# The second layer norm of a mixture-of-experts block, taken one token tile at a time

## What is computed

```python
def layer_norm(x, g, b):
    mu = jnp.mean(xf, -1, keepdims=True)
    var = jnp.mean(jnp.square(xf - mu), -1, keepdims=True)
    return (xf - mu) * lax.rsqrt(var + LN_EPS) * g + b

for l in range(DEPTH):                       # DEPTH = 2
    mix = hybrid_mixer(x, ...)
    x = layer_norm(DEEPNORM_ALPHA * x + mix, ln1_g[l], ln1_b[l])
    moe = hier_moe(x, ...)
    x = layer_norm(DEEPNORM_ALPHA * x + moe, ln2_g[l], ln2_b[l])
return x
```

## Time and profile before

| | |
|---|---|
| median of 3 runs | 1804.32 us (1799.9 to 1805.04) |
| the profiled execution, its own time | 1798.07 us |
| its span | 1795.9 us |
| mean granted TensorE clock | 0.991 |
| TensorE matmul busy | 1741.9 us, 97% |
| VectorE busy | 853.6 us, 48% |
| ScalarE busy | 639.0 us, 36% |
| GpSimd busy | 143.4 us, 8% |

### The profile page before, as it was taken

How to read it: one execution, slowest core, us unless ns; L and a number is a source line. 1 busy time by engine, 2 the same in 40 slices (tenths; PEclk the granted TensorE clock), 3 DMA queues, 4 the chain that set the end, 5 groups by cost and what they waited for, 6 DMA issues and landing times. The chain is left out here.

```text
span 1795.9 us, 24264 instructions
## 1 busy us (share of the span) xinstructions
PE 1741.9 (97%) x9930; PEld 1317.1 (73%) x9930; DVE 853.6 (48%) x1332; ACT 639.0 (36%) x859; POOL 143.4 (8%) x190
## 2 busy tenths in 40 slices
PE   9999999999999999999999999999989999999996
PEld 6888789998988879999888854444458986544442
DVE  6575654445556565444576461122147854312223
ACT  4456443334363544333445221111124541211110
POOL 1020001111111001111110010000002001000000
PEclk9999999999999999999999999999999999999998
DMA  8544545554544454553753169999964506799992
GB/s 302 183 141 148 180 142 188 186 188 168 184 163 141 164 172 158 187 187 117 245 168 117 49 236 399 402 401 396 358 191 148 176 1 245 298 401 399 395 402 110
DMA packets 150941, 396.63 MB, mean 221 GB/s; under 512 B 19376, under 2 KB 83888, under 8 KB 126256
## 3 DMA queue, kind: packets, MB, share of 16 engines
q1 hardware_dynamic: 150832, 395.16, 59.9%
HBM read 394.08 MB, written 1.05 MB: 220 GB/s over the span
## 5 line engine op out<-in xcount | busy, mean ns | idle before, releaser
L803 PE MATMUL ps<-split,split 128*128 128x256 f32 (+3 forms) x1872 | 631.5, 337 | 15.4 <-DVE split L796 4.7
L807 PE MATMUL ps<-split,split 128*128 128x256 f32 (+3 forms) x1872 | 627.9, 335 | 0.6 <-DVE split L2035 0.6
L804 PE MATMUL ps<-split,split 128*128 128x256 f32 (+3 forms) x1872 | 625.0, 334 | 0.0
L781 DVE TENSOR_TENSOR split<-ring,split 128x2048 fp32r<-128x2048 f32 x137 | 314.6, 2304 | 261.7 <-ACT split L774 261.7
L803 PEld LDWEIGHTS ps<-split,split 128*128 128x128 f32 x1872 | 352.4, 188 | 51.2 <-issue 12.0
L807 PEld LDWEIGHTS ps<-split,split 128*128 128x128 f32 x1872 | 352.8, 188 | 34.9 <-DVE split L2035 1.5
L804 PEld LDWEIGHTS ps<-split,split 128*128 128x128 f32 x1872 | 353.9, 189 | 33.1 <-issue 0.5
L774 ACT ACTIVATE split<-ring 128x2048 fp32r<-128x2048 f32 x137 | 262.0, 1916 | 284.6 <-PE ps L807 277.2
L2620 DVE SCALAR_TENSOR_TENSOR arena<-arena,ps 128x256 f32<-128x256 f32 x32 | 15.4, 480 | 226.2 <-ACT arena L1968 226.2
L796 DVE TENSOR_TENSOR split<-ring,split 128x1536 fp32r<-128x1536 f32 (+3 forms) x44 | 80.9, 1852 | 32.1 <-ACT split L790 31.9
L790 ACT ACTIVATE split<-ring 128x1536 fp32r<-128x1536 f32 (+3 forms) x44 | 67.8, 1548 | 76.7 <-PE ps L807 73.2
(11 more groups left out here) (245 smaller groups left out, 2018.2 us busy)
## 6 DMA issues: line engine op xcount, KB each, us to landing
ring<-in_w_in SPq DMA_DIRECT2D x52, 1024.0 KB, 4.9
ring<-in_w_gate_up SPq DMA_DIRECT2D x44, 1024.0 KB, 5.3
ring<-in_expert_w_gate SPq DMA_DIRECT2D x32, 1024.0 KB, 7.7
ring<-in_expert_w_up SPq DMA_DIRECT2D x32, 1024.0 KB, 9.9
ring<-in_expert_w_down SPq DMA_DIRECT2D x32, 1024.0 KB, 10.9
ring<-in_w_down SPq DMA_DIRECT2D x22, 1024.0 KB, 4.9
ring<-in_w_in SPq DMA_DIRECT2D x28, 768.0 KB, 4.7
high<-in_expert_w_gate SPq DMA_DIRECT2D x16, 1024.0 KB, 7.3
```

Source lines behind the costliest of these rows:

```text
L781: nc.vector.tensor_tensor(split(slot), slot, split(high[:, n % HIGH, :]), ALU.subtract).then_inc(low_done.sem, 1)
L803: nc.tensor.matmul(acc, sh, mh, start=start, stop=False)
L804: nc.tensor.matmul(acc, *second, start=False, stop=False)
L807: return nc.tensor.matmul(acc, *third, start=False, stop=stop)
```

## The change

It touches only the second norm. `add_scattered` now holds the four additions, and is called behind the branch: with `last` true in the `If` body. An addition is a `tensor_tensor_reduce`, which also leaves the row's sum; the second half row of a tile starts from the sum of the first. A `tensor_scalar` makes minus the mean of it. ScalarE squares `H - mean` over the whole row, with the sum of squares as by-product. GpSimd makes variance plus epsilon and the power -1/2 for each tile by itself. `second_norm` does both `scalar_tensor_tensor` steps of tile 0 and then both of tile 1, through a buffer `centred` of its own. The idle matmuls at the seam go from 20 to 14. At the tail SP issues `H` in two transfers, one for each tile. Four small buffers are added, and the semaphores change to suit. The first norm keeps its form.

```diff
@@ -482,6 +482,10 @@
         hT = carve(2, 2 * P)
+        centred = carve(TT, D)
+        row_sum = carve(TT, 2)
+        less_mean = carve(TT)
+        square_sum = carve(TT)
 
@@ -554,7 +558,8 @@
         passed = sem("passed")
-        mean_done = signal("mean_done", 2)
+        mean_done = signal("mean_done", 1)
+        mean_in = signal("mean_in", TT)
         table_done = sem("table_done")
@@ -591,9 +596,9 @@
         mix_done = signal("mix_done", 4)
-        stat_done = signal("stat_done", 2)
-        rstd_done = signal("rstd_done", 2)
-        gained = signal("gained", 4)
+        stat_done = signal("stat_done", 1 + TT)
+        rstd_done = signal("rstd_done", 1 + TT)
+        gained = signal("gained", TT)
         wo_in = signal("wo_in", 4)
@@ -619,7 +624,8 @@
         sc_added = signal("sc_added", 4)
-        moe_moments = signal("moe_moments", 4)
+        centred_in = signal("centred_in", TT)
+        squares_in = signal("squares_in", TT)
 
@@ -1006,9 +1012,10 @@
 
-            sp_.wait_ge(x_ready.sem, x_ready.at(LAYERS, 0))
-            sp_.dma_start(out.rearrange("b (t p) d -> (b p) t d", p=P), H[:]).then_inc(out_done, 16)
-            sp_.wait_ge(out_done, 16)
+            for t in range(TT):
+                sp_.wait_ge(x_ready.sem, x_ready.at(LAYERS, t + 1 - TT))
+                sp_.dma_start(out.rearrange("b (t p) d -> (b p) t d", p=P)[:, t, :], H[:, t, :]).then_inc(out_done, 16)
+            sp_.wait_ge(out_done, 16 * TT)
 
@@ -1684,7 +1691,7 @@
                         if l < LAYERS - 1:
-                            keep_running(bank2(("yg", 0, 0, 0)), 20)
+                            keep_running(bank2(("yg", 0, 0, 0)), 14)
                     with pe.Else():
@@ -1991,6 +1998,11 @@
                 more_passes(1)
+                for t in range(TT):
+                    act.wait_ge(mean_in.sem, mean_in.at(l, t + 1))
+                    nc.scalar.activation(flat(XG[1][:, 4 * t:4 * t + 4, :]), H[:, t, :], ACT.Square,
+                                         bias=less_mean[:, t:t + 1],
+                                         accum_out=square_sum[:, t:t + 1]).then_inc(squares_in.sem, 1)
 
@@ -2477,20 +2489,20 @@
 
-                def layer_norm(buf, n):
+                def layer_norm(buf):
 
                     for t in range(TT):
                         last = nc.vector.bn_aggr(mv2[:, t, :], moments2[:, t, :, :])
                     last.then_inc(mean_done.sem, 1)
-                    dve.wait_ge(mean_done.sem, mean_done.at(l, n + 1))
+                    dve.wait_ge(mean_done.sem, mean_done.at(l, 1))
                     nc.vector.tensor_scalar(rstd2, mv2[:, :, 1], LN_EPS, None, ALU.add).then_inc(stat_done.sem, 1)
                     for t in range(TT):
                         nc.vector.scalar_tensor_tensor(out=H[:, t, :], in0=buf[:, t, :], scalar=mv2[:, t, 0:1],
                                                        in1=lng[:, 0, :], op0=ALU.subtract,
                                                        op1=ALU.mult).then_inc(gained.sem, 1)
-                    dve.wait_ge(rstd_done.sem, rstd_done.at(l, n + 1))
+                    dve.wait_ge(rstd_done.sem, rstd_done.at(l, 1))
                     for t in range(TT):
-                        dve.wait_ge(gained.sem, gained.at(l, 2 * n + t + 1))
+                        dve.wait_ge(gained.sem, gained.at(l, t + 1))
                         nc.vector.scalar_tensor_tensor(out=H[:, t, :], in0=H[:, t, :], scalar=rstd2[:, t:t + 1],
@@ -2499,7 +2511,7 @@
                 step(last)
-                layer_norm(H, 0)
+                layer_norm(H)
                 for kp in (1, 3):
@@ -2630,27 +2642,50 @@
                             turned_picks(d + 1)
+                    return passes
+
+                def add_scattered(pass_, last):
+
+                    lp = l * PASSES + pass_
                     dve.wait_ge(resid_in.sem, resid_in.at(l, TT))
+                    if last:
+                        dve.wait_ge(ln2_in.sem, ln2_in.at(l, 32))
+                        dve.sem_inc(passed, 1)
                     for i in range(4):
-                        t, cols = i // 2, slice(i % 2 * 512, (i % 2 + 1) * 512)
-                        nc.vector.tensor_tensor(H[:, t, cols], content_p("sc", i), H[:, t, cols],
-                                                ALU.add).then_inc(sc_added.sem, 1)
-                        dve.wait_ge(sc_added.sem, sc_added.at(lp, i + 1))
-                        moments_of(H, i).then_inc(moe_moments.sem, 1)
-                    return passes
-
-                def second_norm(done):
-
-                    dve.wait_ge(moe_moments.sem, moe_moments.at(PASSES * l + done - 1, 4))
-                    wait_apart(dve, ln2_in.sem, ln2_in.at(l, 32))
-                    layer_norm(H, 1)
+                        t, a = divmod(i, 2)
+                        cols = slice(a * 512, (a + 1) * 512)
+                        key = ("sc", 0, i)
+                        dve.wait_ge(filled[banks2[key]], in_pass(key, l, pass_) + 1)
+                        if a == 1:
+                            dve.wait_ge(sc_added.sem, sc_added.at(lp, i))
+                            dve.sem_inc(passed, 1)
+                        nc.vector.tensor_tensor_reduce(H[:, t, cols], bank2(key), H[:, t, cols], 1.0,
+                                                       0.0 if a == 0 else row_sum[:, t, 0:1], ALU.add, ALU.add,
+                                                       row_sum[:, t, a:a + 1]).then_inc(sc_added.sem, 1)
+                        if last and a == 1:
+                            dve.wait_ge(sc_added.sem, sc_added.at(lp, i + 1))
+                            nc.vector.tensor_scalar(less_mean[:, t:t + 1], row_sum[:, t, 1:2], -1.0 / D, None,
+                                                    ALU.mult).then_inc(mean_in.sem, 1)
+
+                def second_norm():
+
+                    for t in range(TT):
+                        dve.wait_ge(mean_in.sem, mean_in.at(l, t + 1))
+                        nc.vector.scalar_tensor_tensor(out=centred[:, t, :], in0=H[:, t, :], scalar=less_mean[:, t:t + 1],
+                                                       in1=lng[:, 0, :], op0=ALU.add,
+                                                       op1=ALU.mult).then_inc(centred_in.sem, 1)
+                        dve.wait_ge(centred_in.sem, centred_in.at(l, t + 1))
+                        wait_apart(dve, rstd_done.sem, rstd_done.at(l, 1 + t + 1))
+                        nc.vector.scalar_tensor_tensor(out=H[:, t, :], in0=centred[:, t, :], scalar=rstd2[:, t:t + 1],
+                                                       in1=lng[:, 1, :], op0=ALU.mult,
+                                                       op1=ALU.add).then_inc(x_ready.sem, 1)
                     if l < LAYERS - 1:
                         head_low(l + 1)
 
                 def skip_pass(n):
 
                     dve.drain()
-                    for signal_ in (xg_dve, pT_in, h2_done, y_low, sc_added, moe_moments):
+                    for signal_ in (xg_dve, pT_in, h2_done, y_low, sc_added):
                         dve.sem_inc(signal_.sem, n * signal_.per)
@@ -2660,14 +2695,17 @@
                     with dve.If(passes <= done):
-                        second_norm(done)
+                        add_scattered(done - 1, True)
+                        second_norm()
                         skip_pass(PASSES - done)
                     with dve.Else():
+                        add_scattered(done - 1, False)
                         moe_pass(done)
                         if done + 1 < PASSES:
                             more_passes(done + 1)
                         else:
-                            second_norm(PASSES)
+                            add_scattered(done, True)
+                            second_norm()
 
@@ -2770,16 +2808,21 @@
                 diagonal(nm, nm_masked)
-                for n in range(2):
-                    wait_apart(pool, stat_done.sem, stat_done.at(l, n + 1))
-                    nc.gpsimd.tensor_tensor(rstd2, rstd2, minus_half[:, 0:2], ALU.pow).then_inc(rstd_done.sem, 1)
-                    if n == 0:
-                        for t in range(TT):
-                            wait_apart(pool, split_high.sem, split_high.at(l, t + 1))
-                            nc.gpsimd.tensor_tensor(in_blocks(moe_split(H_low[:, t, :])),
-                                                    H[:, t, :].rearrange("p (n k) -> p k n", k=KT),
-                                                    in_blocks(moe_split(H_high[:, t, :])),
-                                                    ALU.subtract).then_inc(split_low.sem, 1)
+                wait_apart(pool, stat_done.sem, stat_done.at(l, 1))
+                nc.gpsimd.tensor_tensor(rstd2, rstd2, minus_half[:, 0:2], ALU.pow).then_inc(rstd_done.sem, 1)
+                for t in range(TT):
+                    wait_apart(pool, split_high.sem, split_high.at(l, t + 1))
```

(11 more changed lines are left out.)

## The result

| | before | after |
|---|---|---|
| median | 1804.43 us (5 runs, 1799.9 to 1805.04) | 1790.67 us (5 runs, 1788.54 to 1791.97) |
| ratio | | 0.9925, 95% interval 0.9911 to 0.9940 |
| profiled execution | 1798.07 us, span 1795.9 | 1789.22 us, span 1787.5 |

The change is faster by 13.8 us, 0.75%. One execution among all that follow, of f3, took 7542.34 us and is left out of its median.

What follows compares the result with a forecast made beforehand. TensorE, busy for 97% of the span, was taken as the bound, leaving two norm stretches of 10.8 us. Tail 2.7 plus seam 1.6 gave 4.3 us; from the median 1804.32, 1800.0 us, range 1794.5 to 1804.5.

Steps and rivals of the forecast that it cites:

- The norm: Second norm at seam and tail: both tiles ready 1.5 us earlier (0.9 to 2.1), tile 0 about 3 us earlier.
- The tail: End of the kernel: 1.5 us from the norm plus 1.2 from the halved output transfer, together 2.7 us (0.9 to 3.4).
- The seam's start: Start of products at the seam: 2.1 us earlier, 1.5 from the norm and 0.6 beyond, worth 1.3 to 2.1.
- The sum behind it: Seam, norm to first product: VectorE's low part of 1.39 us, then a low half of 0.62 twice, about 2.2 us.
- The clock: TensorE at the seam: if its clock falls as before, first products run at 1.2 GHz longer, losing 0.5 to 0.8 us.
- So the whole picture shifts: Behind the seam: VectorE's jump and SP's transfers all come earlier, so 1.6 us arrives further on (-1 to +4).
- the two pauses: VectorE behind the seam's jump: 6.37 us ahead of L2294, 4.69 ahead of L2296, taken as code fetches and expected as before.
- the 4.3 us forecast: Whole kernel: tail's 2.7 us plus seam's 1.6 us, making 1798.07 us 1793.8 for an execution like the profiled one.
- B: Rival at the seam: earlier start lets a fetch precede weight loads, a 4.69 us pause goes; 9.0 us gained, 1795.3; chance 0.17.
- E: Rival, VectorE behind the seam's jump: longer code falls differently into fetches, two more pauses add 11.1 us, 1811.1; chance 0.07.
- The rule on the shared ports: VectorE and GpSimd in the norm: their shared port pair is an exclusive lock, so VectorE would be held up as well.
- Rival D: Both norms: short steps slower than priced, GpSimd holding VectorE 0.55 us each, 2.2 of 4.3 us lost; 1802.1; chance 0.13.

Runs made afterwards that it cites:

- f3: Kernel after with 20 idle matmuls and both centred steps ahead of both last steps on VectorE; 1788.14 us, ratio 0.9925 to before.
- f2: Kernel after with the output in one transfer behind both tiles, as before; 1792.45 us, ratio 0.9946 to before.
- e3: Kernel after with 20 idle matmuls at the seam in place of 14; 1788.43 us, ratio 0.9930 to before.
- e1: Kernel before with 8 VectorE increments added in a never-run branch, moving the code behind the jump; 1797.44 us, ratio 0.9978 to before.
- g2: Kernel before with 3 increments added in the never-run branch; 1797.67 us in a single execution.
- e2: Kernel after with 94 increments added in the never-run branch, landing 128 further on than before; 1796.09 us, ratio 0.9974 to before.
- f4: Kernel after with VectorE waiting for a tile's power ahead of its centred step rather than behind it; 1793.83 us in a single execution.
- f1: Kernel after, unchanged, measured again; 1789.29 us, ratio 0.9931 to before.
- g1: Kernel before with 2 increments added in the never-run branch; 1804.56 us in a single execution.
- g3: Kernel after with VectorE's jump right behind the norm, ahead of the next layer's head, and 40 never-run increments; 1798.24 us in a single execution.

## Why the prediction was wrong

**The norm: right.** Tile 0's mean at T+1.8 (said 1.85), squares at T+1.85, the power of tile 0 held once and over at T+5.15 (the power of tile 1 was held too, 1.37 us, behind steps of VectorE that hid it), tile 0 ready at T+6.56 (6.2 to 6.8), tile 1 at T+9.22 (9.3). ScalarE was in time at both places; its 3.47 us without work at the seam end with the mean, not with code. The squares took 1.15 us and not 1.05, and the addition that starts from a sum 0.75 and not 0.69; both stand in the chain that ended last, and moved it by 0.1 us each at most.

**The tail: right, a little small.** 2.95 us for 2.7: the norm gave 1.6 (said 1.5), the half transfer 1.4 (f2), not 1.2.

**The seam's start: right.** The first product comes 11.28 us after the first addition (1327.87), where it came 13.57 after: 2.3 us, said 2.1. The sum behind it was wrong in one term: the low part of 1.39 us and two low halves of 0.62 make 2.6 us, not the 2.2 stated. The first product came 2.06 us behind the norm, since it waited for one low half only, so the stated figure came out right by luck. The clock fell, as allowed for, and cost 0.7 to 0.9 us (e3), for 0.5 to 0.8 given. What is left of the norm's gain between the marks is less sure than one pair suggests: between kernels without the second pause it is 1.5 us (e1 and after) or 0.9 (g2 and after), between kernels with it 2.5 (before and e2), for 1.6 said.

**The step that failed** is "So the whole picture shifts", in the part on whether the gain arrives further on. I had read the two pauses rightly as code fetched behind the jump, and then took both as fixed furniture which the change would move as one: the term of 1.6 us held nothing for a pause that goes, and it measured 7.35. The second pause was there only because the jump landed three instructions ahead of a border between two pieces of code, and the change lengthens VectorE's code ahead of the landing by 34 instructions, 31 past the border. That is worth 5.8 us in the traces by e1 (4.8 by e2, 6.5 by g2), and with 5.8 the 4.3 us forecast become 10.1; the traces show 10.3, 2.95 + 7.35.

**The rivals.** B had the effect, its place and nearly its price, and a wrong cause: e2 has the full head start, and the pause. E had the right cause, code that "falls differently into what is fetched at once", and looked at it only from the side of loss. What I had in hand and did not use: the program as built shows how many instructions stand ahead of the landing, and rows 9 show the border to the instruction. With pieces of 128, the pause's absence could have been forecast.

The rule on the shared ports showed one of its two directions in the norm. GpSimd is held by a VectorE step with two SBUF operands (0.55 us alone in f4, 1.37 to 1.60 beside one). VectorE's steps beside it kept their 1.27 to 1.29 us in every trace, and f3's pair took 2.47 with the power beside it. Rival D did not occur. The other direction is in the kernel before all the same, beside a GpSimd operation that is long: a VectorE step of 128x8, of which a like one took 0.17 us just before, took 2.72 us while GpSimd worked on 128x1024:

```profile
1051.77 0.17 DVE L2512 SCALAR_TENSOR_TENSOR arena<-arena 128x8 f32<-128x8 f32 x1
1051.97 2.72 DVE L2515 SCALAR_TENSOR_TENSOR arena<-arena 128x8 f32<-128x8 f32 x1
```

```profile
1049.01 5.67 POOL L2779 TENSOR_TENSOR split<-H,split 128x1024 fp32r<-128x1024 f32 x2 [6.79 <-ACT split L1928]
```

**What stays open.** The medians differ by 11.9 us on one occasion and 13.8 on another, the traces by 10.3 between the first mark and the end. Of the rest, 0.4 us is own time beyond the span (2.2 us before, 1.7 after). What remains lies ahead of the seam, where nothing was changed, and where the profiles of the kernels here differ by up to 6.5 us among themselves (first addition from 1314.33 to 1320.86). That part goes with the granted clock. By the trace's record of it, ahead of the seam it was 0.50 for 6.8 us in all in the three profiles of before, e3 and f1, which reach the first addition at 1314.33 to 1315.00, and for 17 to 20.5 us in g1, g2 and g3, which reach it at 1320.43 to 1320.86. TensorE's stretches 240:270 and 670:700, first before, then g1, whose executed code is the same:

```profile
240.00:270.00 30.00, 27.21 (x205) 1.00 0.42 148
670.00:700.00 30.00, 27.22 (x219) 1.00 0.42 141
```

```profile
240.00:270.00 30.00, 27.22 (x191) 0.94 0.42 140
670.00:700.00 30.00, 27.21 (x186) 0.89 0.37 128
```

Why the clock falls there in some executions and not in others was not tried.

## What to carry to other kernels

A jump over code costs a fetch, and what it costs depends on where it lands: one or three instructions ahead of a border it cost two here. When a trace shows an engine idle behind a branch for no reason that the profile names, pad the code that is not run and measure before crediting an edit with the difference; otherwise the layout's 4.8 to 6.5 us would here have been taken for the norm's. For the norm itself the sum from single rows was good to 0.3 us; what was missed was the side effect of the code's length.

## What the runs showed of the hardware

- VectorE's code comes in pieces. The border lies at one instruction (g1, g2), and moving the code by 128 brings it back (e2). The period is 64 or 128 instructions: of its smaller divisors, 32 and 16 would have put the kernel after, 34 further on, where g1 is, with one long pause, and 8 would have left e1 as before. The profile of the kernel after has an instruction queue with 0.30 MB in 37 packets, 8 KB each, and another (q8) with packets of 16 KB:

```profile
q8 instruction: 71, 1.16, 0.3%
q14 instruction: 37, 0.30, 0.1%
```

The Trainium skill (Advanced Engine Details and Errata, section on the ISA cache) gives 256 instructions in a line; with that, a shift of 128 would not have restored the pause, so here the measurement decides for 128 or 64.
- Behind a jump over three passes VectorE stood still for 4.6 to 6.8 us under weight traffic and 3.99 without it (one execution); crossing a border at once costs 4.7 more (4.68 to 4.70 in three traces, and in one pause of 11.05 with the first).
- TensorE's clock can fall although the engine was never idle for more than 1.5 us: around eight transposes of 1.16 us in all, it was at 0.50 from 1326.5 on in the kernel after.
- A short GpSimd operation is stretched from 0.55 to as much as 1.60 us by a long VectorE step beside it and did not hold that step; a GpSimd operation of 2.8 us stretched a VectorE step of 0.17 us to 2.72.
